# Differential attention with the high and low halves of queries and keys stacked along the rows of one product

## The reference

```python
def diff_attend(q1, q2, k1, k2, v, lam):
    scale = DIFF_QK_DIM ** -0.5                       # DIFF_QK_DIM = 32
    s1 = jnp.einsum('bqhd,bkhd->bhqk', q1, k1).astype(jnp.float32) * scale
    s2 = jnp.einsum('bqhd,bkhd->bhqk', q2, k2).astype(jnp.float32) * scale
    p = jax.nn.softmax(s1, axis=-1) - lam * jax.nn.softmax(s2, axis=-1)
    return jnp.einsum('bhqk,bkhd->bqhd', p.astype(v.dtype), v)
```

## Time and profile before

| | us |
|---|---|
| median of 3 runs (3180.12 to 3188.19) | 3185.34 |
| the profiled execution's own time | 3192.75 |
| its span (first to last instruction) | 3191.1 |
| TensorE busy in it | 3002.5 (94%) |
| VectorE busy | 1699.6 (53%) |
| ScalarE busy | 1180.7 (37%) |
| differential attention, layer 0 (first score to last output) | 1579.6 to 1678.9 |
| differential attention, layer 1 | 2601.7 to 2677.1 |
| neighbourhood attention, layer 0 | 1683.4 to 1766.4 |
| neighbourhood attention, layer 1, first score | 2682.0 |

### The profile page before, as it was taken

One profiled execution on the slowest core, in us unless ns is written; L12 is line 12 of the kernel. 1 busy time (PEld: TensorE's weight loads), 2 busy tenths in 40 slices (PEclk: granted clock), 3 DMA queues, 4 the chain that ended last, 5 costly groups with the idle time before them and its releaser, 6 DMA issues.

```text
span 3191.1 us, 40936 instructions
## 1 busy us (share of the span) xinstructions
PE 3002.5 (94%) x16023; PEld 2538.8 (80%) x16023; DVE 1699.6 (53%) x2196; ACT 1180.7 (37%) x1695; POOL 102.5 (3%) x148
## 2 busy tenths in 40 slices
PE   5899999999998999899888989999999988989998
PEld 3788888979786888679787868888886968768886
DVE  4566556454556666464585454555545157354443
ACT  2233333232334333432364343333334235344343
POOL 1000000000000000000000000000000000000000
PEclk7899999999999999999998899999999999999999
DMA  8243434545233444224300212223322230112331
GB/s 279 79 146 109 141 117 127 173 116 161 75 104 108 128 144 145 79 80 126 86 1 1 62 41 91 93 84 100 99 67 80 67 80 1 52 55 91 100 99 66
DMA packets 260449, 307.20 MB, mean 96 GB/s; under 512 B 23467, under 2 KB 231739, under 8 KB 260316
## 3 DMA queue, kind: packets, MB, share of 16 engines
q1 hardware_dynamic: 234716, 224.43, 22.7%
q0 software_dynamic: 19456, 72.00, 7.4%
q10 hardware_dynamic: 6144, 8.91, 0.9%
HBM read 294.05 MB, written 11.27 MB: 96 GB/s over the span
## 4 chain that ended last, share of the span: by engine, by line
PE 88%; DVE 5%; ACT 2%; DVEq 2%; issue 1%; SPq 1%; DMA 1%; ACTq 0%
PE psum L545 25%; PE psum L546 25%; PE psum L547 25%; PE psum L868 3%; PE psum L623 2%; PE psum L878 2%; PE psum L672 1%; PE psum L715 1%; DVE n_t L1578 1%; SPq L436 1%; PE psum L765 1%; DVEq L1577 1%; DVE w_lo L1590 1%; PE psum L702 1%; DMA u_scratch<-u_tab 0%
## 5 line engine op out<-in xcount | busy, mean ns | idle before, releaser
L545 PE MATMUL psum<-hs_hi,w_hi 128*128 128x512 f32 x1632 | 648.5, 397 | 39.8 <-DVE hs_lo L1582 29.3
L1590 DVE TENSOR_TENSOR w_lo<-raw,w_hi 128x2048 fp32r<-128x2048 f32 (+1 forms) x244 | 435.4, 1784 | 464.4 <-ACT w_hi L1057 363.3
L547 PE MATMUL psum<-hs_lo,w_hi 128*128 128x512 f32 x1632 | 641.3, 393 | 0.0
L546 PE MATMUL psum<-hs_hi,w_lo 128*128 128x512 f32 x1632 | 641.2, 393 | 0.0
L545 PEld LDWEIGHTS psum<-hs_hi,w_hi 128*128 128x128 f32 x1632 | 310.7, 190 | 109.6 <-issue 33.1
L547 PEld LDWEIGHTS psum<-hs_lo,w_hi 128*128 128x128 f32 x1632 | 309.8, 190 | 66.2
L546 PEld LDWEIGHTS psum<-hs_hi,w_lo 128*128 128x128 f32 x1632 | 310.7, 190 | 63.8 <-issue 1.0
L1646 DVE SCALAR_TENSOR_TENSOR ada_acc<-ada_raw,csil,ada_acc 128x512 f32<-128x512 f32 x392 | 279.8, 749 | 45.1 <-DMA ada_raw<-in_w_ada 25.7
L545 PE MATMUL psum<-mid_hi,w_hi 128*128 128x512 f32 x768 | 299.3, 390 | 0.0
L546 PE MATMUL psum<-mid_hi,w_lo 128*128 128x512 f32 x768 | 299.1, 390 | 0.0
L547 PE MATMUL psum<-mid_lo,w_hi 128*128 128x512 f32 x768 | 298.8, 389 | 0.0
(11 more groups left out here) (332 smaller groups left out, 5033.9 us busy)
## 6 DMA issues: line engine op xcount, KB each, us to landing
raw<-in_w_in SPq DMA_DIRECT2D x56, 1024.0 KB, 5.2
ada_raw<-in_ada_w POOLq DMA_DIRECT2D x96, 512.0 KB, 4.2
raw<-in_w_ff SPq DMA_DIRECT2D x48, 1024.0 KB, 5.5
raw<-in_w_ff SPq DMA_DIRECT2D x96, 512.0 KB, 3.4
ada_raw<-in_w_ada POOLq DMA_DIRECT2D x32, 512.0 KB, 4.9
raw<-in_w_in SPq DMA_DIRECT2D x24, 512.0 KB, 5.1
ada<-in_w_ada SPq DMA_DIRECT2D x4, 2048.0 KB, 24.0
raw<-in_w_ret_out SPq DMA_DIRECT2D x16, 512.0 KB, 3.4
```

The costliest lines, as they stand in the source:

```text
L545: pe.matmul(dst, lhi, rhi, start=start, stop=False)
L546: pe.matmul(dst, llo, rhi, start=False, stop=False)
L547: return pe.matmul(dst, lhi, rlo, start=False, stop=stop)
L1590: dve.tensor_tensor(w_lo[par][:, 0:kt], raw[par][:, 0:kt], w_hi[par][:, 0:kt].bitcast(F32), ALU.subtract).then_inc(lo_done, 1)
```

## The change

Each half of each head gets its own 128 rows, filled completely: for queries (`qs`, and `qcs` for the context) the rows are high, low, high, low, and for keys (`ks`) high, high, low, low, 32 rows each. One product over these 128 rows is the sum of high x high, low x high, high x low, and also low x low, which was left out before. So `df_score` makes one matmul where `product` made three.

The stacking is done by transfers between on-chip buffers, issued by SyncE: 48 a layer, each of 32 partitions x 2 x 512 or 256 numbers, and 16 more in layer 0 for the context queries. Those of heads 0 and 2 (24) come first and have one semaphore, those of heads 1 and 3 the other. Their sources are whole splits of dfq, dfk, dfkc and dfqc, made once a layer right after the rotation. The stacked buffers lie where `raw`, `w_hi` and `w_lo` are, so units n+9 and n+10 are no longer loaded ahead: all four units of the output matrix are loaded once the last scores are done, and n+9 is split at item 6 of the neighbourhood attention. The zeroed buffers are still needed by the neighbourhood attention; their zeroing moves into VectorE's loop, one after each of items 0 to 3. The split for each head on ScalarE and VectorE is gone.

```diff
@@ sync
-                for j in range(2):
-                    load(n + 9 + j, (n + 9 + j) % 2, cols(wout2[l], 256 * j))
...
+                def stack(dst, c0, w, src, quads, a, half, landed):
+                    r0, t0 = 64 * a + 32 * half, 2 * a + half
+                    for q in quads:
+                        sp.dma_start(dst[32 * q:32 * q + 32, t0:8:4, c0:c0 + w].bitcast(F32),
+                                     src[r0:r0 + 32].bitcast(F32)).then_inc(landed, 16)
+
+                sp.wait_ge(df_split, 4 * l + 3)
+                for a in range(2):
+                    for half in range(2):
+                        stack(ks, 0, S, dfk_hi, (0, 1), a, half, stacked[a])
+                        stack(ks, 0, S, dfk_lo, (2, 3), a, half, stacked[a])
+                        stack(qs, 0, S, dfq_hi, (0, 2), a, half, stacked[a])
+                        stack(qs, 0, S, dfq_lo, (1, 3), a, half, stacked[a])
+                        stack(ks, S, SC, dfkc_hi, (0, 1), a, half, stacked[a])
+                        stack(ks, S, SC, dfkc_lo, (2, 3), a, half, stacked[a])
+                if l == 0:
+                    sp.wait_ge(df_split, 4)
...
+                            stack(qcs, 0, SC, dfqc_hi, (0, 2), a, half, stacked_c)
+                            stack(qcs, 0, SC, dfqc_lo, (1, 3), a, half, stacked_c)
...
-                for j in range(2, 4):
+                sp.wait_ge(df_s, 24 if l == 0 else 40)
+                for j in range(4):
                     load(n + 9 + j, (n + 9 + j) % 2, cols(wout2[l], 256 * j))
@@ tensor
-                pe.wait_ge(df_split, 2 * l + 2)
...
                     if it.pos == 0:
-                        pe.wait_ge(qz_ready, g0 + it.group + 1)
+                        if it.ctx:
+                            pe.wait_ge(stacked_c, 256)
+                        else:
+                            pe.wait_ge(stacked[it.head % 2], 384 * (l + 1))
...
+                        t_ = 2 * it.head + half
+                        q_ = (qcs if it.ctx else qs)[:, t_, tok]
+                        for a_, b_ in ([(S, S + SC)] if it.ctx else [(0, SC), (SC, S + SC)] if half else [(0, S), (S, S + SC)]):
+                            c_ = 768 * half + a_ - (S if it.ctx else 0)
+                            mm = pe.matmul(S3[i % 2][:, c_:c_ + b_ - a_], q_, ks[:, t_, a_:b_], start=True, stop=True)
@@ scalar
-                    if u:
+                    if 0 < u < 8:
                         hi(n + u + 1)
...
+                for j, (whole, part) in enumerate(((dfq, dfq_hi), (dfk, dfk_hi), (dfkc, dfkc_hi), (dfqc, dfqc_hi))[0:4 if wc else 3]):
+                    if j < 2:
+                        act.wait_ge(rot_read, 4 * l + 2 * j + 2)
+                    act.copy(part[:], whole[:]).then_inc(df_hi, 1)
...
+                    if i == 6:
+                        hi(n + 9)
@@ vector
+                    dve.wait_ge(df_hi, 4 * l + j + 1)
+                    dve.tensor_tensor(lo_[:], whole[:], hi_[:].bitcast(F32), ALU.subtract).then_inc(df_split, 1)
...
-                dve.wait_ge(f2_done, 3 if wc else 5)
-                for z in (*qz_hi, *qz_lo):
-                    last = dve.memset(z[:].bitcast(F32), 0.0)
...
+                    if i < 4:
+                        dve.memset((*qz_hi, *qz_lo)[i][:].bitcast(F32), 0.0).then_inc(qz_zero, 1)
...
+                    if i == 6:
+                        lo(n + 9, (n + 9) % 2)
```

More of the change, by code:

```diff
@@ L1424, in _ @@
                     act.mul(y_foc[:], C0[:].rearrange("p (c s) -> p c s", c=2), 2.0 ** 0.5).then_inc(f2_read, 1)
-                act.wait_ge(rot_read, 4 * l + 4)
-                for whole, part in ((dfk, dfk_hi), (dfkc, dfkc_hi)):
-                    act.copy(part[:], whole[:]).then_inc(df_hi, 1)
                 its, i0, g0 = att_items(l)
@@ L1432, in _ @@
                 first_of = [it for it in its if it.pos == 0]
-                def qz_his(it):
-                    c = it.head // 2
-                    for half in range(2):
-                        r_ = slice(HD * (it.head % 2) + DIFF_D * half, HD * (it.head % 2) + DIFF_D * (half + 1))
-                        w_ = SC if it.ctx else S
-                        last = act.copy(qz_hi[it.head % 2][r_, half, 0:w_], (dfqc if it.ctx else dfq)[r_, c, :])
-                    last.then_inc(qzhi_done, 1)
-                act.wait_ge(qz_zero, l + 1)
-                for it in first_of[0:2]:
-                    qz_his(it)
                 def take_pt(i, it, done_t, pt_ok, pv):
@@ L1470, in _ @@
                         df_exps(i + 1, its[i + 1])
-                    if its[i].pos == its[i].size - 1 and its[i].group + 2 < len(first_of):
-                        qz_his(first_of[its[i].group + 2])
                     take_pt(i, its[i], df_t, df_pt, df_pv)
@@ L1997, in _ @@
                     dve.tensor_tensor(src, src, rot_t[j % 2][:], ALU.add).then_inc(rot_read, 1)
+                for j, (whole, lo_, hi_) in enumerate(((dfq, dfq_lo, dfq_hi), (dfk, dfk_lo, dfk_hi), (dfkc, dfkc_lo, dfkc_hi),
+                                                       (dfqc, dfqc_lo, dfqc_hi))[0:4 if wc else 3]):
+                    dve.wait_ge(df_hi, 4 * l + j + 1)
+                    dve.tensor_tensor(lo_[:], whole[:], hi_[:].bitcast(F32), ALU.subtract).then_inc(df_split, 1)
                 dve.wait_ge(lnstd_ready, l + 1)
@@ L2025, in _ @@
                     last.then_inc(sg_out, 1)
-                for j, (whole, lo_, hi_) in enumerate(((dfk, dfk_lo, dfk_hi), (dfkc, dfkc_lo, dfkc_hi))):
-                    dve.wait_ge(df_hi, 2 * l + j + 1)
-                    dve.tensor_tensor(lo_[:], whole[:], hi_[:].bitcast(F32), ALU.subtract).then_inc(df_split, 1)
                 its, i0, g0 = att_items(l)
@@ L2033, in _ @@
                 first_of = [it for it in its if it.pos == 0]
-                def qz_los(it):
-                    dve.wait_ge(qzhi_done, g0 + it.group + 1)
-                    c = it.head // 2
-                    for half in range(2):
-                        r_ = slice(HD * (it.head % 2) + DIFF_D * half, HD * (it.head % 2) + DIFF_D * (half + 1))
-                        w_ = SC if it.ctx else S
-                        last = dve.tensor_tensor(qz_lo[it.head % 2][r_, half, 0:w_], (dfqc if it.ctx else dfq)[r_, c, :],
-                                                 qz_hi[it.head % 2][r_, half, 0:w_].bitcast(F32), ALU.subtract)
-                    last.then_inc(qz_ready, 1)
-                for it in first_of[0:2]:
-                    qz_los(it)
                 def df_max(i, it):
@@ L2105, in _ @@
                         df_max(i + 2, its[i + 2])
-                    if its[i].pos == its[i].size - 1 and its[i].group + 2 < len(first_of):
-                        qz_los(first_of[its[i].group + 2])
                     if ends:
                         df_squares(its[i - 1])
+                    if i < 4:
+                        dve.memset((*qz_hi, *qz_lo)[i][:].bitcast(F32), 0.0).then_inc(qz_zero, 1)
                 df_take(its[-1])
```

30 lines of the change are left out of this document (14 added, 16 removed).

## The result

The changed kernel takes 3193.91 us (median of 20 runs, 3182.27 to 3200.6), the kernel before 3183.88 (20 runs, 3180.12 to 3194.02). The ratio on record is 1.0021 with a 95% interval of 1.0011 to 1.0030: slower by about 7 us (the medians lie 10.0 apart), where 25 us of gain were forecast. The measurement can tell it from no change, but only just.

The account below looks back on a forecast made before the run. TensorE was taken to set the item (4.1 to 4.4 us), VectorE next at 3.18. Gains of 16.8 in layer 0 and 8.2 in layer 1, together 25.0, from the median 3185.34 gave 3160.3 us; range 3151 to 3187.

Parts of the forecast that it names:

- layer 0: first maximum to combine 5: First items of layer 0's differential attention: zeroing there costs VectorE 4.0 us; gain 0.4, less 1.0 for low clock: -0.6.
- layer 0: combine 5 to 13: Two groups of plain latent items in layer 0, at VectorE's 3.18 an item: 34.30 to 28.50 us, gain 5.8.
- layer 0: context items: Layer 0's context items: 1.3 us less waiting and 0.5 for the queries' split, for each of three heads: gain 5.4.
- layer 1: rotation to first maximum: Start of layer 1: transfers come last, landing at 2600.4, gain 1.3; shorter first score adds 2.7: 4.0 us.
- layer 1: neighbourhood attention: Output weights split inside the neighbourhood attention hold up VectorE's queue; bounds 0 and 4, taken as 1.0 us lost a layer.
- Part 1's floors: Plain latent items with one score product: VectorE's 3.18 us and the transposes-copy-values ring's 3.15 limit each item.
- Part 3: Start of layer 0: splits right after the rotation, gate ending at 1575.1, first maximum at 1576.6: gain 7.2 us.
- Part 4, "I take 15": On-chip stacking transfers: first set of 24 lands 15 us after the splits, between bounds of 11.5 plus some 2, and 27.
- My pitch of 0.55: Time from one on-chip transfer's completion to the next: 0.55 us expected, 0.92 in the slow-transfer rival, chance 0.13.
- a sum by bytes (13.0): Estimate for the first 24 transfers: 2.62 MB at 202 GB/s takes 13.0 us.
- "just hidden" for the second set: Second 24 transfers land 28 us after the splits, 1587 and 2613, before item 4's maximum wants them at 1590 and 2616.
- the rival of the clock: TensorE's clock falls to 0.50 in latent items, losing 2.6 us on each affected: 3181 to 3202, put at 3185; chance 0.09.

Follow-up runs that it names:

- e2: The changed kernel, unchanged, run once more for a second trace: ratio 1.0019 to the kernel before, median 3191.89 us.
- e12: e4 with the queries' transfers issued first and the zeroing moved late, no idle transposes where TensorE waits: ratio 0.9988 to the kernel before.
- e6: The changed kernel with idle transposes where TensorE waits, their number also moving the feed-forward loop: ratio 0.9957 to the kernel before, median 3173.25 us.
- e4: The padded kernel: the changed kernel with 56 idle transposes early in the program, which move the feed-forward loop; ratio 0.9982 to before, median 3180.24 us.
- e7: The changed kernel with half of each transfer set issued by ScalarE, plus idle transposes where TensorE waits: ratio 0.9989 to the kernel before.

## Why the prediction was wrong, step by step

| step | forecast gain | measured: after, e2 |
|---|---|---|
| layer 0: rotation to first maximum | 7.2 | 6.7, 6.7 |
| layer 0: first maximum to combine 5 | -0.6 | -2.8, -2.9 |
| layer 0: combine 5 to 13 | 5.8 | 5.2, 4.2 |
| layer 0: context items | 5.4 | 2.3, 3.6 |
| layer 1: rotation to first maximum | 4.0 | 1.8, 1.8 |
| layer 1: first maximum to combine 5 | -0.6 | -2.2, -4.4 |
| layer 1: combine 5 to 13 | 5.8 | 4.5, 4.5 |
| layer 1: combine 13 to the last output | 0 | -5.0, -4.9 |
| layer 1: neighbourhood attention | -1.0 | -1.3, -1.4 |
| feed-forward loop of layer 0 | 0 | -8.1, -6.9 |

(Gains are against the one trace shown of before. The neighbourhood attention of layer 0 took 81 to 91 us, whatever the kernel, so its term isn't measured.)

**Right: Part 1's floors.** Items at 3.18, two groups at 28.8 in the best traces (forecast 28.5).

**Right in number, in part by luck: Part 3.** The gain at the start of layer 0 was 6.7 (forecast 7.2). I had the gate as what ends last, 19.0 behind the rotation, and 1.5 from there to the maximum; in fact the transfers came last, 20.0 behind it, and the maximum came 1.0 later. A later landing and a shorter first score partly cancelled.

**Mis-sized: Part 4, "I take 15".** The first score starts 17.1 and 16.9 after the first issue (1554.77 to 1571.83, 2579.10 to 2596.03), as soon as the first set has landed. My pitch of 0.55 lay between the issue of a plain load, 0.43, and the bias loads; the pitch is 0.64, also for the half-sized ones, which a sum by bytes (13.0) takes at half that: 24 x 0.64 = 15.4, and 1.5 for the last to land. This cost 2 us in layer 1, whose start gained 1.8 instead of 4.0.

**Failed: "just hidden" for the second set.** It landed at 32.3 and 32.2 instead of 28, and it was wanted at 1583.4, 10.6 after the first maximum, not 14: I asked when VectorE's maximum of item 4 is due, but it is TensorE that waits, and it issues these scores two items ahead. Its waits of 3.65 and 2.89 have a low clock behind them: of the 28 to 30 us from the first maximum to combine 5, 14 to 19 ran at 0.50, where the kernel before had at most 1. These distances lost 2.2 to 4.4 where I had put -0.6.

**Half right: the rival of the clock.** I looked for it in the plain items, and there it mostly stayed at 1.00 (in the two traces of the changed kernel 0 to 3.4 us of each c at 0.50). I excluded it in the tail of layer 1 with the earlier trace rows, where transposes and values alone ran at 1.00. But those followed four items with full score work; behind thin items the same work runs at 0.50 in five traces of seven, which costs 5.0. The context items are the other place: I took 5.4 for them, and the five traces without idle turns gain 3.6 at best and lose 3.0 at worst (e12). There the clock didn't fall with the change, it was low already, also around, from which I took the gain; with the clock held they gain 6.3 (e6). The mean of the granted clock over a whole run, in the median of a kernel's runs, is 0.966 to 0.967 for before, 0.957 for the changed kernel, 0.961 for e4, 0.968 for e6.

**Not in the sum: the code's place.** I costed what the instructions do and where they stand, never how many there are ahead of a loop. This is 7 to 8 us, a term that stood at nothing in my sum. With the loop back in 7 blocks the sign turns: the padded kernel is faster than before by 0.18% (about 5 us). That is still far from 25; the rest was lost in the steps above.

**What stays open.** The steps of the table add up to a gain of about 1 (first trace) and of about 0 (second), while the ratio says 7 us slower. The profiled executions of the changed kernel took 3188.56 and 3183.69, less than its median, and stages at a low clock vary from run to run: over its 20 runs the time goes from 3182.27 at a mean clock of 0.959 to 3200.60 at 0.953. Which stages make the missing microseconds, no trace shows. Open too is what lets the clock fall in the context items, in the kernel before as in the changed one.

## What to carry to other kernels

Where a change adds or removes instructions ahead of a loop, look at where the loop lies against the blocks in which the engine loads its code; a few idle instructions can be worth more than the edit. When an engine's work is thinned, ask what its clock does where it already waits: at the starts, in short items, in the tail. And when a transfer is to be hidden, compare its landing with the first engine that waits for it, in that engine's order of issue, not with the last one that needs the result.

## What the runs showed of the hardware that I had not expected

- TensorE's loop of 1664 records ran without code loads where it lay in 7 blocks of 256, and with nine loads a pass and 1.6 to 2.0 us of stall at each jump where it lay in 8. Stall and low clock together cost 3.4 to 4.6 us a jump.
- Transfers between on-chip buffers of 64 rows (32 partitions x 2) take 0.64 us each on one queue, for 64 KB and 128 KB alike; two queues together move 128 KB in 0.64 too, at 201 to 216 GB/s, and 64 KB in less (the second set landed 28 us after the first issue instead of 32).
- Idle transposes that cost TensorE nothing but waiting time held the granted clock at 1.00 in the context items, where it was 0.50 without them, and made the kernel with thin scores some 7 us faster (e4 to e6). Ahead of the first score of the kernel before they gained nothing; elsewhere in it they weren't tried. And they don't always hold it: with the same eight turns the tail of layer 1 was at 1.00 in e7 and for 6.8 us at 0.50 in e6.
